# Merging products on split operands with their loads reordered, and the modulation's weights loaded first, in a one-core layer of a diffusion backbone

## The reference

```python
mod = (silu(cond) @ w_ada + b_ada)                    # 6 parts of 1024, for each of two conditions
sh1, sc1, g1, sh2, sc2, g2 = split(mod, 6)
h = x * (1 + sc1) + sh1
proj = h @ w_in
u_f, rkv, w_dn, a_dn, g_dn, gate_f, gate_r = split(proj)
o_f = fourier_mix(u_f) @ w_fo                         # 512 channels -> 1024
...                                                   # two-way RWKV scan, 16 heads of 64: y, g
o_r = (y * g) @ w_ro                                  # 1024 -> 1024
merged = sigmoid(gate_f) * o_f + sigmoid(gate_r) * o_r
x = layer_norm(alpha * x + g1 * (merged @ w_out))
h2 = x * (1 + sc2) + sh2
aff = softmax(h2 @ w_router)                          # 16 experts, each takes its top tokens: 64 latent, 16 context
x = layer_norm(alpha * x + g2 * experts(h2))          # w_e1, w_e3, w_e2 of every expert
```

## Time and profile before

| what | value |
|---|---|
| time, median of 3 runs | 2687.97 us (2686.44 to 2688.4) |
| time of the profiled execution | 2687.13 us |
| its span (what the trace covers) | 2685.2 us |
| mean granted TensorE clock, as a share of full speed | 0.961 |
| PE busy | 2420.9 us (90% of the span) |
| DVE, ACT, POOL busy | 984.9, 615.4, 363.8 us |
| HBM read | 504.15 MB |

### The profile page before, as it was taken

How to read it: one execution, slowest core, us unless ns; L and a number is a source line. 1 busy time by engine, 2 the same in 40 slices (tenths; PEclk the granted TensorE clock), 3 DMA queues, 4 the chain that set the end, 5 groups by cost and what they waited for, 6 DMA issues and landing times. The chain is left out here.

```text
span 2685.2 us, 58051 instructions
## 1 busy us (share of the span) xinstructions
PE 2420.9 (90%) x26165; PEld 1504.4 (56%) x26165; DVE 984.9 (37%) x1737; ACT 615.4 (23%) x1179; POOL 363.8 (14%) x405
## 2 busy tenths in 40 slices
PE   5999996688998998999689949999999999999993
PEld 3999995577787787788445513333333333333331
DVE  3344311658468467475113431121212212121114
ACT  2122222435535445443200100111111111111111
POOL 0000000315315325224000600000000000000000
PEclk8999998799999999999889969999999999999997
...
GB/s 339 102 242 103 112 112 60 19 20 5 26 25 5 27 25 5 26 8 5 126 238 43 71 291 401 400 394 392 396 396 395 396 394 382 399 396 395 395 294 162
DMA packets 180715, 538.55 MB, mean 201 GB/s; under 512 B 13254, under 2 KB 53926, under 8 KB 180216
## 3 DMA queue, kind: packets, MB, share of 16 engines
...
HBM read 504.15 MB, written 30.70 MB: 199 GB/s over the span
## 5 line engine op out<-in xcount | busy, mean ns | idle before, releaser
L1724 PE MATMUL ps_h_lat<-w_piece,xT 128*64 128x512 f32 x2048 | 456.7, 599 | 8.6 <-DVE hidden L1846 7.5
L1724 PEld LDWEIGHTS ps_h_lat<-w_piece,xT 128*64 128x64 f32 x2048 | 145.7, 138 | 312.9 <-issue 312.9
L1749 PE MATMUL ps_y_lat<-w_piece,hiddenT 128*64 128x512 f32 x1024 | 232.6, 596 | 0.9 <-ACT hiddenT L1610 0.9
L1733 PE MATMUL ps_h_ctx<-w_piece,xT 128*16 128x512 f32 x2048 | 226.1, 593 | 0.0
L1840 DVE TENSOR_TENSOR hidden<-sigmoid_lat,ps_h_lat 64x1024 f32<-64x1024 f32 x32 | 39.1, 1223 | 506.6 <-ACT sigmoid_ctx L1616 506.6
L325 PE MATMUL ps_in<-hT_hi,w_in_hi 128*128 128x320 f32 x752 | 173.3, 312 | 3.0 <-issue 3.0
L666 POOL TENSOR_TENSOR Mo<-x,levels_sb 128x256 f32<-128x256 f32 x200 | 161.9, 832 | 99.2 <-PE ps_scan L908 99.1
L325 PE MATMUL ps_in<-hT_lo,w_in_hi 128*128 128x320 f32 x752 | 172.0, 310 | 0.0
L325 PE MATMUL ps_in<-hT_hi,w_in_lo 128*128 128x320 f32 x752 | 172.0, 310 | 0.0
L908 PE MATMUL ps_scan<-TT_diag,Mo 64*64 64x64 f32 x3200 | 115.0, 220 | 43.8 <-issue 26.6
L1749 PEld LDWEIGHTS ps_y_lat<-w_piece,hiddenT 128*64 128x64 f32 x1024 | 70.2, 137 | 138.3 <-issue 137.7
...
## 6 DMA issues: line engine op xcount, KB each, us to landing
w_piece<-in_w_e SPq DMA_DIRECT2D x192, 2048.0 KB, 13.5
...
```

Source lines behind the costliest of these rows:

```text
L1724: last = pe.matmul(psA[rows, cs], x[:, k, A], w[:, q, cs], start=(k == 0), stop=(k == KD - 1))
L1733: last = pe.matmul(psB[GRP[g], :], x[:, k, B], w[:, q, c * 512:(c + 1) * 512], start=(k == 0), stop=(k == KD - 1))
L1749: last = pe.matmul(psY[rows, :], hT[:, f, A], w[:, q, c * 512:(c + 1) * 512], start=(hf == 0 and f == 0), stop=(hf == 1 and f == FK - 1))
```

## The change

In the front phase both blocks of `w_ada` are loaded before x, each in two halves with a semaphore of its own, so that PE can start on a half. The second block's product goes to another PSUM tensor (`ps_of`), so that it need not wait for `biased(0)`. All of x is turned after the modulation. The eight loads of `b_ada` are issued by ACT, on ACT's own DMA queue.

In the scan phase SP loads the Fourier part (`fT`, 1.3 MB) and the first tile of `w_fo`.

In the merge phase the products are made as in the front phase: ACT rounds weights and inputs (`high_w`, `f_hi`, `y_hi`), DVE subtracts (`low_w`, `f_lo`, `y_lo`), PE adds up three products of 320 columns twice. `yg` is loaded in three pieces. Weights of a column tile are loaded as soon as their buffer is free, `w_out` behind them in two halves, then x and the vectors. The context's modulation vectors come last, and DVE prepares them after the second token tile. The latent softmax and three of eight rounds of the latent choice stand ahead of the context tile's normalisation. PE's `out` of the context tile is cut in three. Two constants of the expert phase are loaded in the merge phase.

```diff
+    KHALF = (slice(0, KD // 2), slice(KD // 2, KD))
...
+        ps_of = lambda r: wide[0] if r == 1 else ps_mod
...
             def load_ada(r):
-                sp.dma_start(w_ada[r % 2][:, :, :], wa_view[:, :, r * RW:(r + 1) * RW]).then_inc(s_wa[r % 2], 16)
+                for ks, landed in zip(KHALF, s_wa[r % 2]):
+                    sp.dma_start(w_ada[r % 2][:, ks, :], wa_view[:, ks, r * RW:(r + 1) * RW]).then_inc(landed, 16)
...
+            load_ada(0)
+            load_ada(1)
             for t in range(NT):
                 src = d["x_sample"][0, t * P:(t + 1) * P, :] if t < CT else d["x_prompt"][0]
                 sp.dma_start(x[:, t, :], src).then_inc(s_x[t], 16)
-            load_ada(0)
-            load_ada(1)
-            b_view = d["b_ada"].rearrange("a (r c n) -> (a c) r n", c=CP, n=CW)
-            for c in range(CP):
-                for j in range(2):
-                    sp.dma_start(bias[32 * c + j:32 * c + j + 1, :, :], b_view[c:c + 1, :, :]).then_inc(s_bias, 16)
             for ch in range(3):
...
             def modulation(r):
-                pe.wait_ge(s_wa[r % 2], 16 * (r // 2) + 16)
-                if r >= 1:
+                if r >= 2:
                     pe.wait_ge(s_mod, r)
                 for k in range(KD):
+                    if k % KHALF[1].start == 0:
+                        pe.wait_ge(s_wa[r % 2][k > 0], 16 * (r // 2) + 16)
                     for c in range(CP):
-                        last = pe.matmul(ps_mod[32 * c:32 * c + 2, 0:CW], cT[:, k, :], w_ada[r % 2][:, k, c * CW:(c + 1) * CW],
+                        last = pe.matmul(ps_of(r)[32 * c:32 * c + 2, 0:CW], cT[:, k, :], w_ada[r % 2][:, k, c * CW:(c + 1) * CW],
...
-            for k in range(3):
-                turn_x(k)
             pe.wait_ge(s_ct, 1)
             modulation(0)
...
-            for k in range(3, KD):
+            for k in range(KD):
                 turn_x(k)
...
             act.activation(sig[:, :], cond[:, :], ACT.Sigmoid).then_inc(s_sig, 1)
+            b_view = d["b_ada"].rearrange("a (r c n) -> (a c) r n", c=CP, n=CW)
+            for c in range(CP):
+                for j in range(2):
+                    act.dma_start(bias[32 * c + j:32 * c + j + 1, :, :], b_view[c:c + 1, :, :]).then_inc(s_bias, 16)
             high(0)
...
             load_rkv(2)
+            sp.dma_start(early[0][:, :, :], d["fT"]).then_inc(s_early, 16)
+            sp.dma_start(early[1][:, :, :], d["w_fo"][0].rearrange("(k p) n -> p k n", p=P)[:, :, 0:P]).then_inc(s_early, 16)
...
-            load(0, 0)
-            sp.dma_start(fT[:, :, :], d["fT"]).then_inc(s_in[0], 16)
-            sp.dma_start(ygT[:, :, :], d["yg"]).then_inc(s_in[1], 16)
...
+            for n, (k0, k1) in enumerate(Y_PARTS):
+                sp.dma_start(y_raw[:, k0:k1, :], d["yg"][:, k0:k1, :]).then_inc(s_in[n], 16)
+            load(1, 0)
+            load(1, 1)
+            for c in range(2):
+                load_gates(c)
+            wo_view = d["w_out"][0].rearrange("(k p) n -> p k n", p=P)
+            for c in range(2, KD):
+                for n in range(2):
+                    sp.wait_ge(s_mm, 2 * (c - 2) + n + 1)
+                    load(c, n)
+                sp.wait_ge(s_mt, c - 1)
+                load_gates(c)
+                if c in (2, 3):
+                    half = slice((c - 2) * KD // 2, (c - 1) * KD // 2)
+                    sp.dma_start(w_out[:, half, :], wo_view[:, half, :]).then_inc(s_wo, 16)
+                if c == 4:
+                    sp.dma_start(w_r[:, :, :], d["w_router"][0].rearrange("(k p) n -> p k n", p=P)).then_inc(s_wo, 16)
+                    for t in range(NT):
+                        src = d["x_sample"][0, t * P:(t + 1) * P, :] if t < CT else d["x_prompt"][0]
+                        sp.dma_start(x1[:, t, :], src).then_inc(s_x, 16)
+                if c == 5:
+                    load_vectors(0, s_vec)
+                    for dst, name in zip(slot_consts, ("iota_slot", "tok_id")):
+                        sp.dma_start(dst[:, :], d[name]).then_inc(s_vec, 16)
+                    sp.dma_start(lng[:, :], d["ln1_g"].to_broadcast([P, DM])).then_inc(s_vec, 16)
+                    sp.dma_start(lnb[:, :], d["ln1_b"].to_broadcast([P, DM])).then_inc(s_vec, 16)
+            sp.wait_ge(s_mm, 2 * KD)
+            load_vectors(1, s_vec1)
             for t in range(NT):
...
+            def high_w(c, n):
+                if c or n:
+                    act.wait_ge(s_w[c % 2][n], 16 * (c // 2 + (c % 2 or n)))
+                act.activation(w_hi[c % 2][n][:, :, :], w_raw[c % 2][n][:, :, :], ACT.Copy).then_inc(s_whi, 1)
+
+            high_w(0, 0)
+            for k in range(FG):
+                act.activation(f_hi[:, k, :], f_raw[:, k, :], ACT.Copy).then_inc(s_fhi, 1)
+            high_w(0, 1)
+            for n, (k0, k1) in enumerate(Y_PARTS):
+                act.wait_ge(s_in[n], 16)
+                for k in range(k0, k1):
+                    act.activation(y_hi[:, k, :], y_raw[:, k, :], ACT.Copy).then_inc(s_yhi, 1)
+            for c in range(1, KD):
+                high_w(c, 0)
+                high_w(c, 1)
+            for t in range(CT):
+                root(t)
                 if t >= 1:
                     turned(t - 1)
-            for n, ts in enumerate(SETS):
-                if n:
-                    turned(CT)
-                act.wait_ge(s_mx, n + 1)
-                act.activation(logit[:, ts, :], logit[:, ts, :], ACT.Exp).then_inc(s_ex, 1)
+            turned(CT - 1)
+            exps(0)
+            root(CT)
+            turned(CT)
+            exps(1)
...
-            pe.wait_ge(s_mt, KD + 2)
-            pe.wait_ge(s_wo, 32)
-            def out(t):
+            for c in range(KD):
+                if c >= 2:
+                    pe.wait_ge(s_mt, c - 1)
+                for n, (kt, x_hi, x_lo) in enumerate(PARTS):
+                    pe.wait_ge(s_wlo, 2 * c + n + 1)
+                    whi, wlo, acc = w_hi[c % 2][n], w_lo[c % 2][n], F[2 * (c % 2) + n]
+                    for k in range(kt):
+                        if c == 0:
+                            pe.wait_ge((s_flo, s_ylo)[n], k + 1)
+                        for p, (w, x) in enumerate(((whi, x_hi), (whi, x_lo), (wlo, x_hi))):
+                            for b in range(2):
+                                last = pe.matmul(acc[:, b * 512:b * 512 + HALF], w[:, k, :], x[:, k, b * HALF:(b + 1) * HALF],
+                                                 start=(k == 0 and p == 0), stop=(k == kt - 1 and p == 2))
+                    last.then_inc(s_mm, 1)
...
+            def affinities(n):
+                pe.wait_ge(s_af, n + 1)
+                for t in range(NT)[SETS[n]]:
+                    last = pe.transpose(F[3][0:NE, t * P:(t + 1) * P], affT[:, t, 0:NE], ident[:, :])
+                last.then_inc(s_at, 1)
+
+            for t in range(CT):
                 out(t)
-                turn(t - 2)
+                if t >= 2:
+                    turn(t - 2)
                 if t >= 3:
                     logits(t - 3)
+            out(CT, ((0, 0, KD),))
+            turn(CT - 2)
+            logits(CT - 3)
             turn(CT - 1)
             logits(CT - 2)
             logits(CT - 1)
+            out(CT, ((1, 0, KD // 2),))
+            affinities(0)
+            out(CT, ((1, KD // 2, KD),))
             turn(CT)
-            for n, ts in enumerate(SETS):
-                pe.wait_ge(s_af, n + 1)
-                for t in range(NT)[ts]:
-                    last = pe.transpose(F[3][0:NE, t * P:(t + 1) * P], affT[:, t, 0:NE], ident[:, :])
-                last.then_inc(s_at, 1)
-                if n == 0:
-                    logits(CT)
+            logits(CT)
+            affinities(1)
...
+            def low_w(c, n):
+                v.wait_ge(s_whi, 2 * c + n + 1)
+                v.tensor_tensor(w_lo[c % 2][n][:, :, :], w_raw[c % 2][n][:, :, :], w_hi[c % 2][n][:, :, :], ALU.subtract).then_inc(s_wlo, 1)
+
+            low_w(0, 0)
+            for k in range(FG):
+                v.wait_ge(s_fhi, k + 1)
+                v.tensor_tensor(f_lo[:, k, :], f_raw[:, k, :], f_hi[:, k, :], ALU.subtract).then_inc(s_flo, 1)
+            low_w(0, 1)
+            for k in range(KD):
+                v.wait_ge(s_yhi, k + 1)
+                v.tensor_tensor(y_lo[:, k, :], y_raw[:, k, :], y_hi[:, k, :], ALU.subtract).then_inc(s_ylo, 1)
+            low_w(1, 0)
+            low_w(1, 1)
...
+            for c in range(KD):
+                v.wait_ge(s_gate[c % 2], 16 * (c // 2) + 16)
+                for n in range(2):
+                    v.wait_ge(s_mm, 2 * c + n + 1)
+                    v.tensor_tensor(split(gate[c % 2][:, n, :]), split(gate[c % 2][:, n, :]),
+                                    split(F[2 * (c % 2) + n][:, :])[:, :, 0:HALF], ALU.mult)
+                v.drain()
+                v.tensor_tensor(mT[:, c, :], gate[c % 2][:, 0, :], gate[c % 2][:, 1, :], ALU.add).then_inc(s_mt, 1)
+                if c + 2 < KD:
```

(17 more changed lines are left out.)

145 lines of the change are left out of this document (68 added, 77 removed).

## The result

| kernel | median | runs | ratio to before | 95% interval |
|---|---|---|---|---|
| before, beside it | 2688.18 us | 4 (2686.44 to 2688.77) | | |
| changed | 2640.7 us | 4 (2638.79 to 2643.13) | 0.9825 | 0.9808 to 0.9842 |

The account below looks back on a forecast made before the run. PE bounds the kernel, and only its waits can shrink: 8.5 (front) + 40.3 (merge) + 1.0 (merge end) + 0.9 (expert start) = 50.7 us off 2687.13 gives 2636.4; with the median 0.84 above, 2637 us, range 2631 to 2643.

Parts of the forecast that it names:

- Front phase: Up to the first products: w_ada ahead of x and an early bias save 8.5 us, ends 5.5 and 9.5.
- rival (a): Front phase: the bias lands with the bulk at 33.60, gain only 5.5 us, time 2640; 8 in 100.
- Merge phase: From the phase's start to out(0): PE runs through, 40.3 us saved, ends 36 and 42.
- pace: Merge phase, seven column tiles: split products take 10.56 us a tile instead of 13.0, saving 17.1 us.
- loads: Merge phase, the rest: 11.83 + 2.8 for the wait and its clock, 8.4 for start and first tile, 23.0 us.
- (b): Merge phase: some column tile waits for its weights, SP's queue being in order; 2642; 12 in 100.
- (c): Merge phase: split products run at low clock, 19.2 us a column tile, slower at 2703; 2 in 100.
- `out` keeps its pace: Merge phase, behind the column tiles: out takes as long as before, change 0.
- End of the merge phase: Up to posT: the new order saves only about 1.0 us, ends -1 and 2.5.
- neither comes back, as PE has no gap there now: Merge phase's end, last latent logits: the 0.48 us wait and about 1.8 us of low clock disappear.
- PE is in a quarter of `out(4)` until 1531.5: Merge phase's end: PE then turns the weights, the copy starts at 1532.2, and DVE's gap is 2.4 us.
- Expert phase: At its start, two DMA issues fewer ahead of w_piece save 0.9 us, ends 0 and 2; the rest unchanged.

Follow-up runs that it names:

- bias_on_sp: The changed kernel with b_ada issued by SP again, behind w_ada and x: 2645.83 us, ratio 0.984, 5.1 over the changed kernel.
- before_new_tail: The kernel before with only the new order at the end of its merge phase: 2691.03 us, ratio 1.0011.
- tail_undone: The changed kernel with the end of its merge phase put back in the order of before: 2636.45 us, ratio 0.9815.
- consts_back: The changed kernel with the two constants (iota_slot, tok_id) loaded at the start of the expert phase again: 2642.52 us, ratio 0.9836.

## Why the prediction was right, and where it was not

**Front phase.** Right in size (8.2 for 8.5) and in kind. The bias on ACT's queue came past the bulk of `w_ada` and landed at least 14.9 us earlier than in SP's queue (before 18.87 against 33.80). The rule of "DMA: Bandwidth & Descriptors" in the Trainium skill (section Queues, rings and completion order), by which the engines take turns between queues, agrees with that. The rule of "Trainium Kernel Development and Optimization" in the Trainium skill (section Key Constraints) is that issuing from several queues only saves issue time; here the issue alone came 15 us earlier (2.52 against 17.52), and "only" does not hold, since the bias also landed ahead of `w_ada` that was issued before it. Read as I had read it, with the bias behind the bulk, the rule would give the time of bias_on_sp, 5.1 us more. My rival (a) priced the late bias at 3 us; 5.7 were measured in the front phase, since h is then made without a head start.

**Merge phase.** Right, 41.1 for 40.3, and term by term: pace 17.4 for 17.1, loads 23.7 for 23.0. PE ran 79.00 of 79.00 us at clock 1.00 behind the first tile, so rivals (b) and (c) are out. "It comes out of a long idle stretch, so at low clock" held as well (0.50 until 1320). The first scan product stands 8.5 us behind the phase's start, 9.3 were computed.

**`out` keeps its pace.** It is 1.7 us shorter in the profile, and nothing shows that to be an effect of the change. `out(0)` follows a wait of 1.92 us in the kernel before, and its clock is 0.66 over the next 4 us. In before_new_tail the same code follows the same 1.92 us at 1.00, and `out` takes 56.1 us as in the changed kernel. The window from 1454 to 1458 in each, the kernel before first:

```profile
1454.00:1458.00 4.00, 3.97 (x6) 1.67 (x7) 3.85 (x4) 0.00 (x0) 0.00 (x0) 0.66 0.00 0
1454.00:1458.00 4.00, 3.57 (x9) 1.66 (x10) 3.85 (x5) 0.00 (x0) 0.00 (x0) 1.00 0.00 0
```

The sum compares with one execution, and a spell of low clock in it was taken as part of the kernel.

**End of the merge phase.** This is the step that failed. The prediction said of the 0.48 wait and the 1.8 of low clock: "neither comes back, as PE has no gap there now", and of the quarter: "PE is in a quarter of `out(4)` until 1531.5". PE had no gap, and the clock fell nevertheless, while PE did turns and 16-column products. Logits took 2.0 us more and the quarter 3.2 more. By the prediction's instants DVE's softmax starts 1528.2 - 1511.85 = 16.35 us after the eviction; it started after 18.52, 2.2 late. The wait for the turned weights was 5.33 us instead of 2.4, 2.9 longer. And the context's logits, which the prediction did not follow, added a wait of 0.65. Together that is the miss of 5.7, and all but the last of it is the low clock. In DVE's gaps: 9.87 + 5.33 + 0.65 + 0.81 = 16.7 us, where the prediction's instants leave 8.9 + 2.4 + 0.8 = 12.1 (before: 8.90 + 2.19 + 1.11 + 0.80 = 13.0). DVE's work from the softmax on took 29.5 us, as computed (29.6). Ahead of it L1526 took 2.81 us, and 1.66 before; why is not known, and it cost nothing, since PE ends the gap behind it.

Without the low clock the new order would have been worth about nothing. An estimate from the rows: a copy at the predicted 1532.2, 20.35 us after the eviction, and the 28.27 us that follow it in the changed kernel make a tail of 48.6, against 49.0 before. The old order lets the context's normalisation hide the turns and logits, at whatever clock they run; the new one lays them bare. tail_undone shows what that costs: 5.1 us of tail, 4.2 between the medians.

**Expert phase.** The issue came 0.9 us earlier as computed, but the first product did not: in this execution it is 0.7 the other way, inside the spread told of at consts_back. So the 5 us between 50.7 and 45.6 are: 5.7 at the end of the merge phase, 1.6 here, 0.6 in the expert phase and 0.3 in the front, less 0.8 in the merge products, 0.7 in the scan and 1.7 in `out`. The last two, 2.4 us, were not computed; that they brought the sum nearer is luck.
